# A fused transformer pair on one core: attention biases in parts, one root for a combined norm, reordered splits

## What is computed

```python
h = x + 0.5 * swiglu(rmsnorm(x, ffn1_norm), ffn1_w1, ffn1_w3, ffn1_w2)
u_pool, q, k, v, g = split(rmsnorm(h, mix_norm) @ w_in)
h = h + concat([pool_mixer(u_pool), retention(q, k, v, g)]) @ w_out
h = h + 0.5 * swiglu(rmsnorm(h, ffn2_norm), ffn2_w1, ffn2_w3, ffn2_w2)
x = rmsnorm(h, final_norm)                       # end of the first layer
parts = split(rmsnorm(x, norm_mix_2) @ w_in_2)   # the second layer
x = x + (sigmoid(g_a) * (y_a @ w_up_a) + sigmoid(g_b) * (y_b @ w_up_b)) @ w_out_2
u, g = split(causal_dwconv(rmsnorm(x, norm_ffn_2) @ w_ffn_in_2))
x = x + (silu(g) * u) @ w_ffn_out_2
out = rmsnorm(x, norm_final_2)
```

## Time and profile before

| | |
|---|---|
| median of 3 runs | 908.35 us (907.44 to 908.43) |
| time of the profiled execution | 908.37 us |
| its span in the profile | 906.4 us |
| granted TensorE clock, mean | 0.994 of 2.4 GHz |
| TensorE busy | 877.6 us, 97% of the span |
| DVE, ACT, GpSimd busy | 650.7, 437.1, 43.0 us |
| read from memory | 154.84 MB, 172 GB/s over the span |

### The profile page before, as it was taken

One profiled execution on the slowest core, in us unless ns is written; L12 is line 12 of the kernel. 1 busy time (PEld: TensorE's weight loads), 2 busy tenths in 40 slices (PEclk: granted clock), 3 DMA queues, 4 the chain that ended last, 5 costly groups with the idle time before them and its releaser, 6 DMA issues.

```text
span 906.4 us, 14183 instructions
## 1 busy us (share of the span) xinstructions
PE 877.6 (97%) x5549; PEld 781.1 (86%) x5553; DVE 650.7 (72%) x831; ACT 437.1 (48%) x551; POOL 43.0 (5%) x47
## 2 busy tenths in 40 slices
PE   8999999999999799999999999999999999999995
PEld 6788888888998688888888899898988999999994
DVE  5776766667767477676676867666876888878876
ACT  6445445444233354444444555556435565555552
POOL 1100000003221000000000100200000000000000
PEclk9999999999999899999999999999999999999999
DMA  8775564655443657556556464524745356465441
GB/s 263 271 235 181 186 202 168 194 177 183 143 140 112 193 183 232 185 185 188 182 185 160 125 180 93 149 93 104 269 140 162 135 165 236 160 211 185 159 142 46
DMA packets 118255, 156.42 MB, mean 173 GB/s; under 512 B 4140, under 2 KB 104028, under 8 KB 118092
## 3 DMA queue, kind: packets, MB, share of 16 engines
q1 hardware_dynamic: 115964, 150.19, 52.1%
q0 software_dynamic: 1152, 4.68, 1.5%
q10 hardware_dynamic: 1104, 1.05, 0.4%
HBM read 154.84 MB, written 1.07 MB: 172 GB/s over the span
## 4 chain that ended last, share of the span: by engine, by line
PE 81%; DVE 11%; ACT 3%; DMA 3%; issue 2%; ACTq 0%; DVEq 0%
PE wk L1442 28%; PE acc L1550 20%; PE wk L1467 16%; PE wk L1465 8%; DVE w_lo L835 3%; DMA raw<-in_ffn_w 2%; PE wk L1798 1%; ACT w_hi L428 1%; PE acc L1770 1%; PE acc L1474 1%; ACT w_hi L435 1%; DVE xhl L846 1%; PE acc L1783 1%; DVE w_lo L841 1%; DMA raw<-in_w_in 1%
## 5 line engine op out<-in xcount | busy, mean ns | idle before, releaser
L1442 PE MATMUL wk<-xhl,w_hi 128*128 128x256 f32 x1472 | 272.6, 287 | 1.9 <-DVE arena L1150 1.7
L1467 PE MATMUL wk<-xhl,w_hi 128*128 128x512 f32 x704 | 251.6, 400 | 0.0
L841 DVE TENSOR_TENSOR w_lo<-raw,w_hi 128x2048 fp32r<-128x2048 f32 x83 | 190.0, 2289 | 80.5 <-ACT w_hi L435 80.0
L1442 PEld LDWEIGHTS wk<-xhl,w_hi 128*128 128x128 f32 x1472 | 230.2, 192 | 6.5 <-issue 4.7
L1442 PE MATMUL wk<-xhl,w_lo 128*128 128x256 f32 x736 | 208.1, 283 | 0.0
L1465 PE MATMUL wk<-xhl,w_lo 128*128 128x256 f32 x704 | 199.8, 284 | 6.4 <-DVE xhl L846 5.0
L435 ACT ACTIVATE w_hi<-raw 128x2048 fp32r<-128x2048 f32 x83 | 157.9, 1904 | 26.9 <-PE wk L1442 26.9
L1467 PEld LDWEIGHTS wk<-xhl,w_hi 128*128 128x128 f32 x704 | 133.4, 189 | 32.0
L1550 PE MATMUL acc<-w_hi,hhl 128*128 128x512 f32 x480 | 153.6, 391 | 1.2 <-DVE w_lo L841 1.2
L428 ACT ACTIVATE w_hi<-raw 128x2048 fp32r<-128x2048 f32 x56 | 106.4, 1908 | 75.5 <-PE wk L1442 49.5
L835 DVE TENSOR_TENSOR w_lo<-raw,w_hi 128x2048 fp32r<-128x2048 f32 x56 | 129.8, 2324 | 18.1 <-ACT w_hi L428 17.8
(11 more groups left out here) (257 smaller groups left out, 925.9 us busy)
## 6 DMA issues: line engine op xcount, KB each, us to landing
raw<-in_ffn_w SPq DMA_DIRECT2D x65, 1024.0 KB, 5.3
raw<-in_w_in SPq DMA_DIRECT2D x26, 1024.0 KB, 6.6
raw<-in_w_ffn_in SPq DMA_DIRECT2D x22, 1024.0 KB, 5.1
raw<-in_w_ffn_out SPq DMA_DIRECT2D x11, 1024.0 KB, 4.8
raw<-in_w_out SPq DMA_DIRECT2D x8, 1024.0 KB, 4.9
arena<-bias_scratch POOLq DMA_DIRECT2D x1, 2048.0 KB, 13.4
raw<-in_cmp_w_k SPq DMA_DIRECT2D x2, 1024.0 KB, 5.3
raw<-in_cmp_w_v SPq DMA_DIRECT2D x2, 1024.0 KB, 5.3
```

The lines of the kernel that those rows point to most:

```text
L841: nc.vector.tensor_tensor(w_lo[:, s], raw[:, s], w_hi[:, s].bitcast(F32), ALU.subtract) \
L1442: mm = nc.tensor.matmul(dst, w, v, start=start and n == 0, stop=stop and n == len(pairs) - 1, skip_group_check=True)
L1467: return nc.tensor.matmul(bank, wh[:, c, cols], xhl[:, c].rearrange("p n t -> p (n t)"), start=False, stop=c == DC - 1, skip_group_check=True)
```

## The change

Seven edits:

1. **Biases.** GpSimd's `first_gain` and `bias` loads no longer stand behind the heads. They wait for the second feed-forward: the gain for its first `hl_out`, and the bias in four DMAs of four heads (512 KB) each, one for each of the four turns that follow. The three memsets behind them now stand in front. DVE's first use waits for all four (`16 * 4`).
2. **Norms.** The squares are scaled by 1/sqrt(D) in the activation, so that mean and EPS take one DVE step (`mean_square`) where there were two; the last step of the root writes its target, which saves the copy.
3. **Combined norm.** `rstd_both` takes one root over four columns where it took two roots over two; `spread(3)` on TensorE stands half a unit earlier.
4. **Swaps and rope.** `swap_halves(0)` moves from the end of mixer unit 1 into the middle of unit 2; `rope(m - 2)` stands before `proj(m)`.
5. **Output units.** `lo(U_OUT1 + 2)` moves ahead of the heads' gating; the first gate product moves ahead of the last projection.
6. **Up units.** `lo(U_UP + 3)` moves behind `y_lo_part(3)`.
7. **Opening.** 8 + 3 + 2 products of zeros where there were 5 + 2, and the transposes of x pairs 2 and 3 stand before chunks 1 and 3, where they stood before chunks 2 and 4.

```diff
@@ GpSimd
             pool.wait_ge(head_lo, 2)
-            nc.gpsimd.dma_start(first_gain, a["final_norm"].partition_broadcast(P)).then_inc(first_gain_in, 16)
-            pool.wait_ge(bias_written, 16)
-            nc.gpsimd.dma_start(bias, bass.AP(tensor=scratch.tensor, offset=0,
-                                              ap=[[1, P], [BIASW, 16], [1, T]])).then_inc(bias_ready, 16)
             for z in kz:
                 nc.gpsimd.memset(z, 0.0).then_inc(kz_zero, 1)
             nc.gpsimd.memset(blk, 0.0).then_inc(blk_zero, 1)
+            pool.wait_ge(hl_out, FI + 1)
+            nc.gpsimd.dma_start(first_gain, a["final_norm"].partition_broadcast(P)).then_inc(first_gain_in, 16)
+            pool.wait_ge(bias_written, 16)
+            for j in range(4):
+                pool.wait_ge(hl_out, FI + 2 + j)
+                nc.gpsimd.dma_start(bias[:, 4 * j:4 * j + 4],
+                                    bass.AP(tensor=scratch.tensor, offset=4 * j * BIASW,
+                                            ap=[[1, P], [BIASW, 4], [1, T]])).then_inc(bias_ready, 16)
@@ DVE
+            def mean_square(n):
+
+                dve.wait_ge(sq_ready, BANKS * (n + 1))
+                step(nc.vector.scalar_tensor_tensor(out=nr[:, 0, 0:2], in0=sums_x[:, 0], scalar=EPS, in1=sums_x[:, 1],
+                                                    op0=ALU.add, op1=ALU.add))
...
-                step(nc.vector.tensor_tensor(v, sums_x[:, 0], sums_x[:, 1], ALU.add))
-                step(nc.vector.tensor_scalar(v, v, 1.0 / D, EPS, ALU.mult, ALU.add))
-                r = rsqrt(2)
-                step(nc.vector.tensor_copy(first_r[:], r))
-                step(nc.vector.tensor_tensor(v, first_r[:], first_r[:], ALU.mult))
+                mean_square(3)
                 dve.wait_ge(xf_sq, 2)
-                step(nc.vector.tensor_tensor(v, v, sums_f[:], ALU.mult))
-                step(nc.vector.tensor_scalar(v, v, 1.0 / D, EPS, ALU.mult, ALU.add))
-                r = rsqrt(2)
-                step(nc.vector.tensor_tensor(rstd_t[:], first_r[:], r, ALU.mult))
-                spread_diag()
+                step(nc.vector.scalar_tensor_tensor(out=nr[:, 0, 2:4], in0=nr[:, 0, 0:2], scalar=EPS, in1=sums_f[:],
+                                                    op0=ALU.mult, op1=ALU.add))
+                rsqrt(4, both_r[:])
+                spread_diag(both_r[:, 2:4])
                 lo(U_IN2 + 2)
...
-                proj(m)
+                    gate_mult(0)
                 if 2 <= m < 6:
                     rope(m - 2)
+                proj(m)
...
-            for j in range(2):
-                dve.wait_ge(gate_tanh, j + 1)
-                step(nc.vector.scalar_tensor_tensor(out=g_t[:, j], in0=g_t[:, j], scalar=1.0, in1=g_s[:, j],
-                                                    op0=ALU.add, op1=ALU.mult))
+            lo(U_OUT1 + 2)
+            gate_mult(1)
             dve.wait_ge(hspread_ready, 1)
...
-            lo(U_UP + 3)
...
             y_lo_part(2)
             y_lo_part(3)
+            lo(U_UP + 3)
             lo(U_UP + 4)
@@ TensorE
-                keep_warm(5)
+                keep_warm(8)
...
-                for p in range(5):
-                    if p < 4:
-                        pe.wait_ge(x_in[p], 16)
-                        turn_pair(0, p)
-                    if p == 0:
-                        keep_warm(2)
-                        continue
...
+                pe.wait_ge(x_in[0], 16)
+                turn_pair(0, 0)
+                keep_warm(3)
+                pe.wait_ge(x_in[1], 16)
+                turn_pair(0, 1)
+                keep_warm(2)
+                for c in range(DC):
+                    if c in (1, 3):
+                        pe.wait_ge(x_in[c // 2 + 2], 16)
+                        turn_pair(0, c // 2 + 2)
...
+                    elif m == 2:
+                        swap_halves(0)
...
-                if 1 <= m < 5:
+                if 2 <= m < 5:
                     swap_halves(m - 1)
...
-                    if at == (1, 1):
                         spread(3, wk[:, 3, T:])
```

More of the change, by code:

```diff
@@ L588, in _ @@
                 act.wait_ge(xf_ready, tt + 1)
-                nc.scalar.activation(xf[:, tt], xf[:, tt], ACT.Square, accum_out=sums_f[:, tt:tt + 1]) \
+                nc.scalar.activation(xf[:, tt], xf[:, tt], ACT.Square, scale=D ** -0.5, accum_out=sums_f[:, tt:tt + 1]) \
                     .then_inc(xf_sq, 1)
@@ L862, in handoff, with rsqrt @@
                     x_lo(c, n, gain)
-            def rsqrt(n):
+            def rsqrt(n, out=None):
                 v, r, t = (nr[:, j, 0:n] for j in range(3))
@@ L869, in rsqrt, with spread_diag @@
                                              ALU.mult, ALU.add))
-                for _ in range(3):
+                for n_step in range(3):
                     step(nc.vector.scalar_tensor_tensor(out=t, in0=r, scalar=-0.5, in1=r, op0=ALU.mult, op1=ALU.mult))
                     step(nc.vector.tensor_tensor(t, t, v, ALU.mult))
-                    step(nc.vector.scalar_tensor_tensor(out=r, in0=t, scalar=1.5, in1=r, op0=ALU.add, op1=ALU.mult))
-                return r
+                    dst = out if out is not None and n_step == 2 else r
+                    step(nc.vector.scalar_tensor_tensor(out=dst, in0=t, scalar=1.5, in1=r, op0=ALU.add, op1=ALU.mult))
+                return r
+            def mean_square(n):
+                dve.wait_ge(sq_ready, BANKS * (n + 1))
+                step(nc.vector.scalar_tensor_tensor(out=nr[:, 0, 0:2], in0=sums_x[:, 0], scalar=EPS, in1=sums_x[:, 1],
+                                                    op0=ALU.add, op1=ALU.add))
             def rstd_diag(n):
-                dve.wait_ge(sq_ready, BANKS * (n + 1))
-                v = nr[:, 0, 0:2]
-                step(nc.vector.tensor_tensor(v, sums_x[:, 0], sums_x[:, 1], ALU.add))
-                step(nc.vector.tensor_scalar(v, v, 1.0 / D, EPS, ALU.mult, ALU.add))
-                r = rsqrt(2)
-                step(nc.vector.tensor_copy(rstd_t[:], r))
-                spread_diag()
-            def spread_diag():
+                mean_square(n)
+                rsqrt(2, rstd_t[:])
+                spread_diag(rstd_t)
+            def spread_diag(rows):
                 for tt in range(2):
-                    nc.vector.tensor_scalar(diag[:, tt], ident, rstd_t[:, tt:tt + 1], None, ALU.mult) \
+                    nc.vector.tensor_scalar(diag[:, tt], ident, rows[:, tt:tt + 1], None, ALU.mult) \
                         .then_inc(diag_ready, 1)
@@ L1076, in decay, with gate_mult @@
                     .then_inc(st_out, 1)
+            def gate_mult(j):
+                dve.wait_ge(gate_tanh, j + 1)
+                step(nc.vector.scalar_tensor_tensor(out=g_t[:, j], in0=g_t[:, j], scalar=1.0, in1=g_s[:, j],
+                                                    op0=ALU.add, op1=ALU.mult))
             for m in range(10):
@@ L1118, in _ @@
                                         mh[:, 4 + 2 * j:6 + 2 * j].bitcast(F32), ALU.subtract).then_inc(head_lo, 1)
-            for m in range(3):
+            for m in range(1, 3):
                 lo(U_OUT1 + m + 2)
@@ L1422, in _ @@
                 add_residual(5, b, 0.5)
-            dve.wait_ge(sq_ready, BANKS * 5 + BANKS)
-            v = nr[:, 0, 0:2]
-            step(nc.vector.tensor_tensor(v, sums_x[:, 0], sums_x[:, 1], ALU.add))
-            step(nc.vector.tensor_scalar(v, v, 1.0 / D, EPS, ALU.mult, ALU.add))
+            mean_square(5)
             r = rsqrt(2)
@@ L1497, in opening_unit @@
                 nc.tensor.transpose(wk[:, 2, 0:DC], vec_rows[0:DC], ident[0:DC, 0:DC]).then_inc(gain_turned, 1)
-                for p in range(5):
-                    if p < 4:
-                        pe.wait_ge(x_in[p], 16)
-                        turn_pair(0, p)
-                    if p == 0:
-                        keep_warm(2)
-                        continue
-                    pe.wait_ge(lo_done if p == 4 else lo_first, 1 if p == 4 else p)
-                    for c in (2 * p - 2, 2 * p - 1):
-                        pe.wait_ge(xl_ready, c + 1)
-                        for t in range(2):
-                            mm = split_chunk(wh, wl, c, t, wk[:, t])
+                pe.wait_ge(x_in[0], 16)
[8 more added lines that the diff above has]
+                        turn_pair(0, c // 2 + 2)
+                    pe.wait_ge(lo_first if c < 6 else lo_done, c // 2 + 1 if c < 6 else 1)
+                    pe.wait_ge(xl_ready, c + 1)
+                    for t in range(2):
+                        mm = split_chunk(wh, wl, c, t, wk[:, t])
                 return mm
```

14 lines of the change are left out of this document (4 added, 10 removed).

## The result

The changed kernel takes 895.18 us (median of 4 runs, 894.80 to 896.43) against 908.12 us (907.44 to 908.43): 12.9 us less. The recorded ratio of the two is 0.9866 with a 95% interval of 0.9847 to 0.9884 (the two medians alone give 0.9858). The forecast was 894.9, with a range of 892.0 to 899.5. The profiled execution is the slowest of the four, 896.43 us with a span of 894.3.

A forecast was written before the change was run, and what follows sets the result against it. TensorE, 97% busy, was taken to bound the kernel, so gains had to come from its few waits. Terms summed to 13.6 us, reduced by 0.1 to 13.5: from 908.4 to 894.9 us, range 892.0 to 899.5.

The forecast's parts named there:

- handoff wait, slow clock, output split: Handoff to second feed-forward and output units: TensorE's wait of 5.0 us, half-rate clock 2.1 and split wait 1.4 go.
- combined norm: Seam before U_IN2+2: 13 small steps instead of 29 and an earlier spread end TensorE's projection wait, -1.65 us.
- opening: Kernel start: TensorE's transposes held ACT back; earlier ones give -0.95 us, bounds 0 (later loads pace the start) and -2.2.
- the 0.1 for the spreads: Whole sum: 13.6 us reduced by 0.1 for spreads that now interrupt a unit.
- either would do: Handoff to second feed-forward: earlier split of U_OUT1+2 or moved bias copy, each alone enough to end the 5.0 us wait.
- Nothing else is late next: Handoff to second feed-forward: no other late operand follows once the wait is gone, so the full 5.0 us go.
- The clock term: Behind the handoff: without the stall, 4.2 us at granted clock 0.50 hold 2.1 us of full-rate work, -2.1 us.
- Thin covers: Rival: heads, up(3), third feed-forward's chain and opening each give less, 1.5 to 3.5 us off, about 897.4; chance 0.13.
- More at the opening: Rival: longer zeros end half-rate first chunks sooner, or slow clock took more; 1 to 2 us earlier, 893.0; chance 0.14.
- Handoff stays: Rival: something besides bias load and late issue kept x_hi back, so 7.1 us stay, 902.0; chance 0.08.
- No effect: Rival: the waits return behind TensorE's later units and the gain is given back, 908; chance 0.04.
- Slower by the bias parts: Rival: bias parts hold up unit loads in the second feed-forward's loop, up to 919.3 us; chance 0.04.

The follow-up runs named there:

- both undone: Changed kernel with the 2 MB bias load and the split of U_OUT1+2 both back behind the heads: 903.02 us.
- spread late: Changed kernel with the combined norm's spread back at the end of unit U_IN2+1, the one root kept: 897.86 us.
- the three runs: Changed kernel with the whole bias behind the heads again, 895.77 us; with the split of U_OUT1+2 late, 897.65 us; with both, 903.02 us.

## Why the prediction was right

| term | forecast | measured, from |
|---|---|---|
| handoff wait, slow clock, output split | 8.5 | 8.8, both undone (8.16 + 0.61) |
| combined norm | 1.65 | 1.76 in B, 1.65 of it the wait, spread late |
| up units | 1.0 | 0.93 |
| rope | 0.5 | 0.76 |
| roots: second, third feed-forward, end | 0.4, 0.4, 0.2 | 0.38, 0.42, 0.18 |
| bias in parts | 0 | 0 |
| opening | 0.95 | 0 as far as the scatter lets one see; the profiled execution lost 1.0 |

Without the opening the forecast's terms are 12.55 us after the 0.1 for the spreads. Before and after differ by 285.42 - 275.55 = 9.87 in A and 583.05 - 579.81 = 3.24 in B, together 13.1. With the 1.0 us that the opening lost this makes the 12.1 of the profiled spans (906.4 - 894.3). The medians differ by 12.9.

**The handoff** went as the prediction had it, down to the load of 5 to 6 us (5.4), and "either would do" is shown by the three runs. The 8.8 are what is left after a new wait of 0.22 that I had not seen coming: with ScalarE and the load out of the way, what is late next is the split of U_FFN2+1, which stands behind the splits of x on VectorE. "Nothing else is late next" was not quite so.

**The clock term** of 2.1 us is inside the 8.8. The Trainium skill (TensorE: Matmul & The Clock Gate, "What's actually happening") has the count of slow products vary from run to run. The opening bears that out: four products of 0.63 us in one execution, and one of 0.49 in another, with the same order. Behind the handoff the two profiled executions that have the stall agree, 0.50 through 307.4 to 311.6 in both. No run takes the slow clock away and keeps the stall, so the 2.1 us are read from the row, and only the sum of 8.8 is measured.

**The combined norm**: the size was right, the reason half told. I derived it from the shorter root and let the spread's place follow. The two runs say that neither does it alone: without the earlier place the shorter root gives 0, and without the shorter root the earlier place gives 0.75 of 1.76.

**The opening** is the term that was mis-sized, at 0.95 and measured at 0. Its step "TensorE's transposes held ACT back" took one execution's late start for the order's doing. The bound of 0 that I had given it, "if later loads pace the start", is what happens, and x's own loads, which the prediction left out, hold the moved transposes as well: in the changed kernel's profile ScalarE waits for three loads in a row (0.54, 0.29 and 0.66 us), the last of them here.

```profile
24.48 1.92 ACT L428 ACTIVATE w_hi<-raw 128x2048 fp32r<-128x2048 f32 x1 [0.66 <-DMA raw<-in_ffn_w]
```

That the median still came within 0.3 us of the forecast is luck in part: the 0.95 that is missing is made up by 0.6 us that handoff and rope gave beyond their terms, and by the new median of before, 908.12 where the forecast had started from 908.37. None of this was forecast.

**The rivals.** Thin covers: both of 0.2 us held, at the heads (line 1110 waits 0.23 for TensorE, not for the split) and at `up(3)` (no wait there on TensorE's list), and so did the third feed-forward's chain (0.42). Of the four places that it named only the opening failed. More at the opening: out. Of the 12 profiled executions with the new opening one has a product of 0.63 us among the first unit's wide ones, so the slow ones at the start may have become rarer, but no time was gained by it. Handoff stays: out. No effect: out, since A and B are both shorter. Slower by the bias parts: its mechanism is there, a load held to 10.9 us, but the price was wrong, since the price took the thinnest cover of the turn for all of it. The whole bias in one piece costs nothing there. Not tested alone are the moves of the first gate product and of `swap_halves(0)`, both forecast at 0.

## What to carry over

When a wait has several conditions, undo them one at a time and then together; here the single runs said 0.0 and 1.7 us, the pair 8.2. A spread, broadcast or other small product that another engine waits for belongs at the first place where its input is ready, in the middle of a unit if need be, and shortening the work ahead of it pays only as far as it makes that place possible. For terms under one us compare stretches between marks that the kernels share, since they repeat to 0.2 to 0.4 us where whole executions scatter by 1 to 9, look for the row that grew, since one late load moved such a stretch by 1.1 us, and never price a kernel's opening from one execution.

## What the hardware did unexpectedly

TensorE's clock fell while the engine was busy without a gap. In the changed kernel's timeline the rows from 21.91 to 25.07, right ahead of the fall, are small products:

```profile
21.91 0.81 PE L1650 MATMUL acc<-arena 32*16 32x384 f32 x2
22.66 0.30 PE L1654 MATMUL acc<-cst,arena 96*128 96x96 f32 x1
22.89 0.44 PE L1656 MATMUL acc<-cst,arena 44*128 44x44 f32 x4
23.26 1.97 PE L1663 MATMUL acc<-arena 128*128 128x32 f32 x16
...
25.78 0.63 PE L1468 MATMUL wk<-xhl,w_hi 128*128 128x512 f32 x1
```

The busy time is 4.00 of 4.00 us from 20 to 24, yet the granted clock is 0.50 from 25.2, and the product of 128x512 at 25.78 takes 0.63 us where those before 21.9 took 0.39. All kernels here have these small products, and in 5 of 14 profiled executions the clock fell behind them. That they are the cause is an inference from the order of the rows; no run took them away.
